# Attention values and two probability tiles per head turned in 32x32 blocks and through DRAM, on one Trainium2 core

## What is computed

```python
p = jax.nn.softmax(logits, axis=-1)          # diff: p[:, 0] - lam * p[:, 1]
out = jnp.einsum('bhqk,bkhd->bqhd', p, v)
```

## Time and profile before

| | |
|---|---|
| median of 3 runs | 1644.09 us (1641.63 to 1644.32) |
| the profiled execution, its own time | 1643.9 us |
| its span, first to last instruction | 1642.1 us |
| PE busy | 1612.4 us, 98% |
| DVE, ACT, POOL busy | 1202.8, 902.5, 903.1 us |
| mean granted TensorE clock | 0.997 |

### The profile page before, as it was taken

How to read it: one execution, slowest core, us unless ns; L and a number is a source line. 1 busy time by engine, 2 the same in 40 slices (tenths; PEclk the granted TensorE clock), 3 DMA queues, 4 the chain that set the end, 5 groups by cost and what they waited for, 6 DMA issues and landing times.

```text
span 1642.1 us, 32437 instructions
## 1 busy us (share of the span) xinstructions
PE 1612.4 (98%) x12028; PEld 1563.2 (95%) x12028; DVE 1202.8 (73%) x2233; ACT 902.5 (55%) x1776; POOL 903.1 (55%) x703
## 2 busy tenths in 40 slices
PE   9999999999999999999999999999999999999998
PEld 8989999999999999999999999899999999999997
DVE  5666655656656799889897789634357998898977
ACT  4365545454546665565565445644367655655654
POOL 4453445364544067677575547664450676775754
PEclk9999999999999999999999999999999999999999
DMA  6221223343422223423323332344242233233232
GB/s 189 81 64 53 67 78 86 77 108 77 112 75 68 65 78 92 115 71 111 97 84 90 89 81 70 92 120 110 64 110 60 78 94 112 74 107 98 84 91 71
DMA packets 283008, 145.50 MB, mean 89 GB/s; under 512 B 60591, under 2 KB 273261, under 8 KB 282853
## 3 DMA queue, kind: packets, MB, share of 16 engines
q1 hardware_dynamic: 278392, 136.27, 30.1%
q0 software_dynamic: 3616, 6.92, 1.6%
q10 hardware_dynamic: 844, 0.24, 0.1%
HBM read 130.69 MB, written 15.32 MB: 89 GB/s over the span
## 4 chain that ended last, share of the span: by engine, by line
PE 81%; DVE 11%; ACT 3%; issue 3%; POOL 1%; DMA 0%; POOLq 0%; ACTq 0%; DVEq 0%
PE ACC L1444 29%; PE ACC L1883 11%; PE ACC L1884 11%; PE ACC L1885 11%; PE ACC L1724 2%; PE S L1699 2%; PE S L1885 2%; PE S L1883 2%; PE S L1884 2%; DVE SCO L3137 2%; DVE TOP L3134 1%; PE T L1444 1%; ACT PR L2335 1%; PE T L1712 1%; PE S L1673 1%
## 5 line engine op out<-in xcount | busy, mean ns | idle before, releaser
L3645 POOL TENSOR_TENSOR WL<-RAW,WH 128x1024 fp32r<-128x1024 f32 (+3 forms) x89 | 187.8, 2114 | 147.2 <-ACT WH L2210 147.0
L1444 PE MATMUL ACC<-XGh,WH 128*128 128x288 f32 (+1 forms) x1008 | 227.6, 307 | 6.3 <-DVE XGl L2828 1.8
L1444 PE MATMUL ACC<-XGh,WL 128*128 128x288 f32 (+1 forms) x1008 | 215.3, 295 | 0.0
L1444 PE MATMUL ACC<-XGl,WH 128*128 128x288 f32 (+1 forms) x1008 | 215.3, 295 | 0.0
L1883 PE MATMUL ACC<-TB,WH 128*128 128x288 f32 x640 | 188.5, 295 | 1.4 <-DVE TB L3355 1.4
L1885 PE MATMUL ACC<-TB,WL 128*128 128x288 f32 x640 | 188.6, 295 | 0.0
L1884 PE MATMUL ACC<-TB,WH 128*128 128x288 f32 x640 | 188.3, 294 | 0.0
L2493 ACT ACTIVATE TC<-ACC 128x288 f32<-128x288 f32 x192 | 79.0, 411 | 167.7 <-PE ACC L1885 167.0
L1444 PEld LDWEIGHTS ACC<-XGh,WH 128*128 128x128 f32 (+1 forms) x1008 | 159.0, 188 | 11.4 <-issue 4.0
L1444 PEld LDWEIGHTS ACC<-XGh,WL 128*128 128x128 f32 (+1 forms) x1008 | 161.6, 188 | 0.0
L1444 PEld LDWEIGHTS ACC<-XGl,WH 128*128 128x128 f32 (+1 forms) x1008 | 161.3, 187 | 0.0
(11 more groups left out here) (517 smaller groups left out, 5244.2 us busy)
## 6 DMA issues: line engine op xcount, KB each, us to landing
RAW<-in_w_gate_dram SPq DMA_DIRECT2D x44, 512.0 KB, 3.9
RAW<-in_w_up_dram SPq DMA_DIRECT2D x44, 512.0 KB, 5.0
RAW<-in_w_down_dram SPq DMA_DIRECT2D x48, 384.0 KB, 3.8
RAW<-in_w_in_even_dram SPq DMA_DIRECT2D x29, 512.0 KB, 5.2
RAW<-in_w_in_odd_dram SPq DMA_DIRECT2D x28, 512.0 KB, 4.6
RAW<-in_w_out_even_dram SPq DMA_DIRECT2D x16, 512.0 KB, 4.2
RAW<-in_w_down_dram SPq DMA_DIRECT2D x16, 256.0 KB, 2.9
RAW<-in_w_out_odd_dram SPq DMA_DIRECT2D x8, 512.0 KB, 5.1
```

The source lines that it names most:

```text
L1444: ins = pe.matmul(out[0:m, 512 * b:512 * b + width], left, right[:, b * width:(b + 1) * width], start=(first and part == 0), stop=(last an ...
L3645: pool.tensor_tensor(WL[slot][:, 0:n], RAW[slot][:, 0:n], WH[slot][:, 0:n].bitcast(F32), ALU.subtract).then_inc(w_lo_pool, 1)
```

## The change

For the values of all diff and dsa heads but 16 (`blockwise`), PE's five transpositions and DVE's two copies go. DVE turns the projected values in 32x32 blocks in slot 0 (`turn_values`, slot 1 for head 17) into a new tile VT; SP stores VT to the output with eight DMAs of 128-byte runs, as for the keys, and after the weights of the head's other slots loads the rows back into VF (`load_values`, two DMAs); the job "v" waits for these.

For query tiles 2 and 3 of 13 heads (8 to 14, 17 to 22), `turn_probs`, and with it the reading of PSUM, goes. DVE turns the probabilities in blocks right after the next `row_maxima` (`probs_to_blocks`, slots 3 and 4); SP stores each tile to the memory of the output `y_prompt` (four DMAs of 128-byte runs), waits, and loads it turned (one DMA of 512-byte runs) into PF; ACT takes the high part in slots 5 and 7 (`loaded_hi`), DVE the low part in slot 6 and in slot 0 of the next head (`loaded_lo`). PE's turn of tile 4 stays in slot 6, ACT's and DVE's part of it moves to slot 7. SP issues the next head's loads of slots 0 and 1 ahead of the stores and waits of the blocks. In heads whose slot 1 has an unfinished projection, `weighted_values(h - 1)` comes after its first k tile.

The diff, cut to its core:

```diff
+BLOCK_TILES = (2, 3)
+BLOCK_HEADS = (8, 9, 10, 11, 12, 13, 14, 17, 18, 19, 20, 21, 22)
+def blockwise(g):
+    return kind_of(g) != "mla" and g != 16
+def last_turn(h):
+    return 1 + TOK_TILES if h in BLOCK_HEADS else 2 + TOK_TILES
...
 # SP, store_keys(g), after the keys
+                if blockwise(g):
+                    sp.wait_ge(vals_made, value_loads(g) // 32 + 1)
+                    for name, b0, b1 in (("_prompt", 0, SEQ // SQUARE), ("_sample", SEQ // SQUARE, NT // SQUARE)):
+                        tokens = outs[dst + name][:, c].rearrange("(b t) (q d) -> q t b d", t=SQUARE, d=SQUARE)
+                        for q in range(QUADRANTS):
+                            sp.dma_start(tokens[q], VT[q * SQUARE:(q + 1) * SQUARE, b0:b1, :]).then_inc(vf_out, 16)
+                    return
...
+            def load_values(g):
+                sp.wait_ge(vf_out, value_stores(g + 1))
+                sp.wait_ge(job_lo, jobs.made("v", g - 1))
+                sp.dma_start(VF[:, 0:QT, :], outs[dst + "_prompt"][:, c].rearrange("(t p) d -> p t d", p=P)).then_inc(vf_in, 16)
+                sp.dma_start(VF[0:DEC, QT, :], outs[dst + "_sample"][:, c]).then_inc(vf_in, 16)
+            def store_blocks(h, t):
+                sp.wait_ge(pb_made, block_number(h, t) + 1)
+                if b:
+                    sp.wait_ge(pf_in[t], 16 * b)
+                for q in range(QUADRANTS):
+                    dst = bass.AP(place, first + q * SQUARE, [[P, SQUARE], [P * SQUARE, QUADRANTS * (t + 1)], [1, SQUARE]])
+                    sp.dma_start(dst, PB[t][q * SQUARE:(q + 1) * SQUARE, 0:(t + 1) * P].rearrange(
+                        "p (b q) -> p b q", q=SQUARE)).then_inc(pb_out[t], 16)
+            def load_turned(h, t):
+                sp.wait_ge(pb_out[t], 16 * QUADRANTS * (b + 1))
+                if b:
+                    sp.wait_ge(pf_lo, block_number(BLOCK_HEADS[b - 1], t) + 1)
+                src = bass.AP(place, first, [[P, P], [P * P, t + 1], [1, P]])
+                sp.dma_start(PF[t][:, :, :], src).then_inc(pf_in[t], 16)
+            def turn_through_memory(h):
+                load_next("slot", h + 1, 0)
+                load_next("slot", h + 1, 1)
+                for t in BLOCK_TILES:
+                    store_blocks(h, t)
+                    load_turned(h, t)
 # SP, attention(h)
-                    load_next("slot", h, s)
+                    if s > 1 or h - 1 not in BLOCK_HEADS:
+                        load_next("slot", h, s)
+                if blockwise(h):
+                    load_values(h)
+                if h in BLOCK_HEADS:
+                    turn_through_memory(h)
...
 # PE
+            def values_late(h):
+                c = share(h, 1)
+                return h > 8 and blockwise(h) and c is not None and c[3] < c[4]
...
                 pe.wait_ge(t_free, tr.made("p", h, QT))
+                if h in BLOCK_HEADS:
+                    pe.wait_ge(pf_lo, block_number(h, BLOCK_TILES[-1]) + 1)
...
-                    if 2 <= s < 2 + TOK_TILES and (h, s) != (16, 6):
+                    if 2 <= s < last_turn(h) and (h, s) != (16, 6) and not in_blocks(h, s - 2):
                         turn_probs(h, s - 2)
+                    if s == 1 and not blockwise(h):
+                        values_to_tokens(h)
                     if s == 1:
-                        values_to_tokens(h)
-                        if h % 16:
+                        if h % 16 and not values_late(h):
                             weighted_values(h - 1)
...
+                    elif s == 1 and values_late(h):
+                        prepare(*c[:2], c[2], c[2] + 1)
+                        weighted_values(h - 1)
+                        prepare(*c[:2], c[2] + 1, c[3])
...
 # ACT
+            def loaded_hi(h, t):
+                act.wait_ge(pf_in[t], 16 * (BLOCK_HEADS.index(h) + 1))
+                act.wait_ge(acc_done, acc.made("pv", h - 1))
+                act.activation(PTh[:, 0:t + 1, t * P:(t + 1) * P], PF[t][:, :, :], ACT.Copy).then_inc(pf_hi, 1)
...
 # DVE
+            def probs_to_blocks(h, t):
+                dve.wait_ge(*probs_made(h, t))
+                dve.transpose(PB[t][:, 0:w], PR[0][:, n % 2, 0:w]).then_inc(pb_made, 1)
+            def loaded_lo(h, t):
+                dve.wait_ge(pf_hi, block_number(h, t) + 1)
+                dve.tensor_tensor(PTl[:, 0:t + 1, cols], PF[t][:, :, :],
+                                  PTh[:, 0:t + 1, cols].bitcast(F32), ALU.subtract).then_inc(pf_lo, 1)
...
                         row_maxima(h, s)
+                    if s and in_blocks(h, s - 1):
+                        probs_to_blocks(h, s - 1)
...
+                    if s == (1 if h == 17 else 0) and blockwise(h):
+                        turn_values(h)
+                    if s == 0 and h - 1 in BLOCK_HEADS:
+                        loaded_lo(h - 1, 3)
...
+                    if s == 6 and h in BLOCK_HEADS:
+                        loaded_lo(h, 2)
```

More of the change, by code:

```diff
@@ L148, in early_output, with value_stores, value_loads, in_blocks @@
     return h - 1 if h % 2 and kind_of(h) == "dsa" else None
+def blockwise(g):
+    return kind_of(g) != "mla" and g != 16
+def value_stores(g):
+    return 16 * sum(2 * QUADRANTS if blockwise(i) else 2 for i in range(8, g))
+def value_loads(g):
+    return 16 * 2 * sum(blockwise(i) for i in range(8, g))
+BLOCK_TILES = (2, 3)
+BLOCK_HEADS = (8, 9, 10, 11, 12, 13, 14, 17, 18, 19, 20, 21, 22)
+def in_blocks(h, t):
+    return h in BLOCK_HEADS and t in BLOCK_TILES
+def last_turn(h):
+    return 1 + TOK_TILES if h in BLOCK_HEADS else 2 + TOK_TILES
+def block_number(h, t):
+    return BLOCK_HEADS.index(h) * len(BLOCK_TILES) + BLOCK_TILES.index(t)
 def q_job_slot(g):
@@ L386, in plan_attention @@
                     scores(("s", h, s, m), m if k == "diff" else s % 2)
-            if 2 <= s < 2 + TOK_TILES and (h, s) != (16, 6):
+            if 2 <= s < 2 + TOK_TILES and (h, s) != (16, 6) and not in_blocks(h, s - 2):
                 tr.add("p", h, s - 2)
@@ L393, in plan_attention @@
             if s == 1:
-                tr.add("v", h)
-                tr.add("v5", h)
+                if not blockwise(h):
+                    tr.add("v", h)
+                    tr.add("v5", h)
                 if h % 16:
@@ L826, in build @@
         assert e <= own
+        (PB2, PF2, PF3), e = overlay(e, ("PB2", [P, 3 * P], F32), ("PF2", [P, 3, P], F32), ("PF3", [P, 4, P], F32))
+        assert e <= own
+        (PB3,), e = overlay(sq_off + size([P, NT], F32), ("PB3", [P, SEQ], F32))
+        PB, PF = {2: PB2, 3: PB3}, {2: PF2, 3: PF3}
         (QIh, QIl), end3 = overlay(end3, ("QIh", [P, 4, NT], F32R), ("QIl", [P, 4, NT], F32R))
@@ L908, in build @@
         pt_hi = sem("pt_hi")
+        pb_made, pf_hi, pf_lo = (sem(n) for n in ("pb_made", "pf_hi", "pf_lo"))
+        pb_out, pf_in = ({t: sem(f"{n}{t}") for t in BLOCK_TILES} for n in ("pb_out", "pf_in"))
         b_sq, rb_sqrt = sem("b_sq"), sem("rb_sqrt")
@@ new lines, in load_turned @@
+            def load_turned(h, t):
+                b = BLOCK_HEADS.index(h)
+                sp.wait_ge(pb_out[t], 16 * QUADRANTS * (b + 1))
+                if b:
+                    sp.wait_ge(pf_lo, block_number(BLOCK_HEADS[b - 1], t) + 1)
+                place, first = turned_place(t)
+                src = bass.AP(place, first, [[P, P], [P * P, t + 1], [1, P]])
[6 more added lines that the diff above has]
+                    load_turned(h, t)
@@ L1284, in job_source @@
                 return acc_free, acc.made(w, g)
+            if w == "v" and blockwise(g):
+                return vf_in, value_loads(g + 1)
             if w == "v":
@@ L2329, in exponents @@
                 if n >= 2:
-                    act.wait_ge(t_done, tr.made("p", *divmod(n - 2, TOK_TILES)))
+                    before = divmod(n - 2, TOK_TILES)
+                    if in_blocks(*before):
+                        act.wait_ge(pb_made, block_number(*before) + 1)
+                    else:
+                        act.wait_ge(t_done, tr.made("p", *before))
                 if h == 16 and t == 0:
@@ L2376, in attention @@
                         job("k", g)
-                    if 2 <= s < 2 + TOK_TILES and (h, s) not in ((15, 5), (16, 4)):
+                    if 2 <= s < last_turn(h) and (h, s) not in ((15, 5), (16, 4)) and not in_blocks(h, s - 2):
                         turned_hi(h, s - 2)
+                    if s == 7 and h in BLOCK_HEADS:
+                        turned_hi(h, QT)
                     if h in OUTPUT_FIRST and s == 2:
@@ L3172, in attention @@
                         take_keys(h)
-                    if s == 1 and h != 16:
+                    if s == (1 if h == 17 else 0) and blockwise(h):
+                        turn_values(h)
+                    if s == 1 and not blockwise(h) and h != 16:
                         take_values(h)
@@ L3178, in attention @@
                         evacuate(("wo", *out_tile(h, s)), add_to_x(out_tile(h, s)[1]))
-                    if 2 <= s < 2 + TOK_TILES:
```

(7 more changed lines are left out.)

46 lines of the change are left out of this document (34 added, 12 removed).

## The result

The median after is 1645.12 us over 20 executions (1640.78 to 1649.55), before, on the same chip, 1642.53 over 20 (1641.47 to 1644.34): a ratio of 1.0015, 95% interval 1.0009 to 1.0021. That is 2.5 us slower, where 2.9 us faster was forecast; it lies within the range of 1628 to 1653 and within 0.2% of no change, but beyond its own interval, on the other side. The executions are spread over 8.8 us, for 2.9 before. The profiled one took 1644.83 us, 0.9 more than the profiled one of before (1643.9), which was itself 1.4 us above the median of before.

What follows compares the result with a forecast made beforehand. PE's own work was taken to bound the kernel. Savings -15.6, heads 22 and 23 +8, clock +1.7, head 17 +2, ACT +1 make -2.9 us against 1643.9: 1641.0 us, range 1628 to 1653 for 8 in 10.

Steps and rivals of the forecast that it cites:

- The saving where nothing is late: PE without the transpositions of values (0.52 us), tile 2 (0.30) and tile 3 (0.44): 1.26 us saved per head.
- Head 17 as a late trip: Head 17's blocks come back through memory after PE wants them: a wait of 1.3 us, taken as 2 (0 to 4).
- In head 23 ACT was held by the load of VF: Head 23: VF lands at about 1236, so ACT's high part and the last tile's exponents come 8.5 us late.
- The landing of 128-byte runs: DMA queues: a 64 KB store in 128-byte runs lands 3.0 us after issue; later than 4 would refute the forecast.
- the rival of the choking queues: DMA queues: many small packets slow landings from 3.0 to 4.6 us, making the kernel slower, priced at 1659; chance 0.20.
- at 1665: Choking queues: time if landings cost +15 us in sum and about 1 us in each of ten other heads.
- Savings of 9.3 us in heads 8 to 15: First layer's share of the 17.4 us saved on PE: values 0.52 us a head, tiles 2 and 3 0.30 and 0.44.
- I charge 1 us for all of it: ACT, held 3 to 6 us for tile 2 in slot 5 of heads 8, 18 and 20, costs 1 us (0 to 3).
- The rival "held": Every head: ACT or DVE, held behind a load, turns PE's saving into waits; 1641 to 1648, no change; chance 0.10.
- I count nothing, since in all heads but two they are due several us ahead of PE: DVE's low parts, 26 with two SBUF inputs, could be blocked by GpSimd up to 42 us in sum; priced at nothing.
- The clock, 1.7 us, once, near 1225: PE's granted clock falls to near 0.5 for 3.4 us behind head 22's long wait: 1.7 us (0 to 3.4).
- Heads 22 and 23, 8 us, of which 7 at the product of 22: SP's queue is too long: product of 22 7.0 us late, 23's 8.5, overlapping; 8 us taken (5.5 to 12).

Runs made afterwards that it cites:

- trim: The change, but TensorE again turns the probability tiles of heads 17, 21 and 22 and the values of 23: 1633.67 us, 0.9941 to the kernel before.
- trim_wait: `trim` plus a wait of TensorE before head 18's product for an otherwise unused 64 KB load: 1638.59 us, 0.9973 to the kernel before.
- the order changed: `trim` with head 21's tiles in blocks again and head 22's values turned in slot 1, behind the low part: 1636.28 us, 0.9963 to the kernel before.

## Why the prediction was wrong

**Right.** The saving where nothing is late: heads 18 to 20 gave 1.3 us each for 1.26. Head 17 as a late trip: its wait was 2.55 us for 2, and without the value stores in SP's queue it is not there. In head 23 ACT was held by the load of VF, as forecast. The landing of 128-byte runs: 2.3 us for a block store of 64 KB, 2.0 for a value store, 3.4 for a key store (3.0 before), all below the 4.4 from which the rival of the choking queues decides, and `trim` settles it. (Its price "at 1665" is a slip: the terms given, 15 us and 1 us in each of ten heads, make 1669. The sum did not use it.)

**Wrong, in four terms.**

- *Savings of 9.3 us in heads 8 to 15, and "I charge 1 us for all of it" for ACT held in slot 5.* Of the 9.3 us, 8.8 lie in the row from product 7 to 15. The profile gave 3.8 there, and nine other profiles of the same code 4.6 to 6.0. PE's own work fell by 7.5 us, and 3.7 went into new idle time: 0.5 us at 275.5 behind DVE's row maxima, where PE arrives 0.5 sooner (the whole saving of head 8's values), and 0.7 to 1.0 us each at 297, 365 and 503. Behind these three stands the trip: at 297 by the chain shown above, and at 365 and 503 GpSimd's MIXl (the low part of the output projection's operand) waits for ACT's MIXh, which comes right behind a high part of tile 3 that had waited 3.2 and 2.0 us for its load. So ACT was held as forecast, 5.6 us in head 8, but what was queued behind it on ACT and DVE did not have that much time. Without the trip of the tiles the same stretch gave 7.0 us. The rival "held" had this mechanism, with a chance of 0.10 and for every head; it is true of the first layer in part. The last 1.8 of the 8.8 us are not the tiles' trip: the values alone leave as much out (1.7 of 3.6 us came). In the profile without that trip 0.5 us more stand behind the row maxima and 0.8 behind DVE's copy of a head's result to BO, which comes after a mixing of 2.41 us beside a GpSimd split, as in the earlier trace rows; the rest is open.
- *"I count nothing, since in all heads but two they are due several us ahead of PE."* The low part of tile 3 is due with no margin in head 21, because head 22's slots 0 and 1 stand next to each other on PE. It took 1.98 us there, and PE waited 3.19. The row that warned of it was the earlier trace rows. By the rule of the Trainium skill (SBUF — State Buffer, SBUF: two separate sides) that I cited and then priced at nothing, a DVE instruction with two SBUF inputs and a GpSimd instruction that reads SBUF exclude each other for a whole instruction. The trace agrees: this low part ended 0.56 us after GpSimd's split did, and alone it takes 0.65 to 0.69. The row 20 to 21 should have shrunk by 1.3 us (and by 0.8 more for the shift) and grew by 1.2: 3.2 us lost. No wait at all was forecast for this head.
- *The clock, 1.7 us, once, near 1225.* In the profiled execution it fell at 1210 for 8 us and at 1230 for 6, some 4 us of work (5.86 x 0.42 + 5.50 x 0.28). Other executions lose it elsewhere: the one without head 22's tiles has 0.80 over 8 us from 1068 and 0.62 from 1196, behind waits of 2.96 and 3.13 us. The median's share is estimated above at 5.3 us, and by that estimate this term alone turns -2.9 into +0.7. `trim_wait` measured one added wait: 5.3 us (uncertain by 2.7) for 2.2.
- *Heads 22 and 23, 8 us, of which 7 at the product of 22.* The total is nearly right, and in part by luck. Their two rows grew by 6.8 us with 1.3 of saving in them, so 8.1 were lost. But 5.6 of that are waits (0.58, 3.20 and 1.82), where "some 9 us" in one wait were forecast, and the rest is mostly the lower clock, which the forecast had as a term of its own. The place is not right: SP issued the keys in 4.0 us for 5.2, and no wait stands before the product of 22 itself. PE waited before it for X, behind DVE's low part of tile 2, which waits for ACT, which waits for the load, and later for the values of 23. I had followed SP's queue to the product, and not who is queued behind the waiting instruction on ACT and DVE. It is the same omission as in the first term.

Summed against the profiled execution, from the table of intervals: -3.8 in heads 8 to 15 (counted -8.8, and +1 for ACT), -3.8 in 18 to 20, +1.4 at 17, +1.2 at 21, +6.8 in 22 and 23, +1.7 in the tail (a lower clock at its beginning is part of it; the rest is open), and -2.5 in the two stretches that the change hardly touches: +0.9. The forecast of -2.9 was for this execution. Of the 5.4 us between -2.9 and the +2.5 of the medians, 1.4 are that the profiled execution of before, from which the sum started, was slower than its median of 20; the forecast took it to be 0.2 below the median.

What stays open: why the same wait is followed by a lower clock in one execution and not in another; what head 21's wait costs; and the price of head 22's tiles, which came out as 0.8 us, less than the uncertainty.

## What to carry to other kernels

Price a wait of a saturated TensorE at its length plus what the clock takes behind it, and list all waits before you sum the savings. When an engine is held by a load, look at each instruction queued behind it, and behind the engines that wait for it, and when TensorE wants that one. Here a trip that saves 0.5 to 0.7 us per head must never be late, and a few late ones among 28 (15 of values, 13 of tiles) cost all that the others gain. Use such a detour only in the places where the trace leaves room, and take the others out one by one: the same idea, in fewer heads, is 11 us faster than before instead of 2.5 slower. When an engine gets an instruction with two SBUF inputs, look what GpSimd runs at that moment in each place where the result is due at once.

## What the runs showed of the hardware

- A wait of 2.19 us of a TensorE that had been busy without pause for the 25 us before, for a 64 KB load that nothing else used, was followed by a mean grant of 0.70 over 5.7 us; the time grew by 5.3 us, uncertain by 2.7. Behind a wait of 3.1 to 3.2 us before the product of head 21 the grant was 0.62 over 8.9 us, 0.50 over 5.3 and 0.60 over 3.9 in the profiles of three kernels, and stayed at 1.00 in those of two.
- A DVE subtraction of 128x512 with both inputs in SBUF took 0.65 to 0.69 us alone. Beside a GpSimd subtraction that had begun earlier it ended 0.56 us after that one's end, whenever it had started: 1195.09 after 1194.53 in the profile after (GpSimd 1192.17 + 2.36), 1191.85 after 1191.29 with the order changed (1188.95 + 2.34). For the low parts of tile 3 that started while GpSimd was splitting a WL, it is 0.55 to 0.57 us in the profiles of eight kernels, with one exception, 0.67, where DVE started 0.02 us before GpSimd's end. So it does nearly all its work after GpSimd is done; the time it takes is the rest of GpSimd's instruction plus nearly its own.
- Stores of 64 KB in 128-byte runs landed in 2.0 us (values), 2.3 (blocks) and 3.4 (keys), medians of the profile after; loads of blocks, 192 and 256 KB, in 2.6 and 2.9, loads of values, 256 KB, in 3.6 to 3.7.
